# Attention of a two-part transformer block on one core: two heads per item, scores on row halves, values in column halves, outputs written in place, and one chain for both kinds of attention in layer 2

## The reference, cut to what matters

```python
# dilated (layer 1)
scores = einsum('bdhnqe,bdhnke->bdhnqk', qb, kw) * e ** -0.5   # and -inf outside the pattern
p = exp(scores - mx); den = sum(p); o = einsum('bdhnqk,bdhnke->bdhnqe', p, vw) / den
# windowed (layer 2)
p = exp(s - m); p = p / (sum(p) + exp(sk - m)); o = einsum('bnhgqk,bnkhd->bnqhgd', p, vb)
# neighbourhood (layer 2)
p = softmax(s + bias); o = einsum('bhqrk,brkhd->bqhd', p, vr)
# each followed by a product with an output matrix; q and k are normalised over their 64 values before
```

## Time and profile before

| | |
|---|---|
| median of 3 runs | 2544.2 us (2543.84 to 2547.39) |
| profiled execution, its own time | 2548.99 us |
| its span in the trace | 2547.3 us |
| TensorE matmul busy | 2474.9 us, 97% |
| VectorE busy | 1314.4 us, 52% |
| ScalarE busy | 929.2 us, 36% |
| dilated attention in the trace | from 74 to 352 us |
| both attentions of layer 2 | from 1134 to 1359 us |

### The profile page before, as it was taken

One profiled execution on the slowest core, in us unless ns is written; L12 is line 12 of the kernel. 1 busy time (PEld: TensorE's weight loads), 2 busy tenths in 40 slices (PEclk: granted clock), 3 DMA queues, 4 the chain that ended last, 5 costly groups with the idle time before them and its releaser, 6 DMA issues.

```text
span 2547.3 us, 32783 instructions
## 1 busy us (share of the span) xinstructions
PE 2474.9 (97%) x12740; PEld 1943.1 (76%) x12740; DVE 1314.4 (52%) x2069; ACT 929.2 (36%) x1463; POOL 55.0 (2%) x131
## 2 busy tenths in 40 slices
PE   8999999988999999999999999999999999999999
PEld 6777777776788888876667888887777876888887
DVE  5555555666654433557556443355565465534433
ACT  5433454334433322445445332243232232423322
POOL 3000000000000000040000000000000000000000
PEclk9999999999999999999999999999999999999999
DMA  4222213211223323320102333332222221433332
GB/s 147 70 64 64 70 60 91 62 59 51 91 91 102 97 91 99 99 87 22 46 30 92 99 99 91 95 103 83 67 67 83 75 70 34 120 94 105 92 96 76
DMA packets 60640, 205.79 MB, mean 81 GB/s; under 512 B 7249, under 2 KB 7249, under 8 KB 60386
## 3 DMA queue, kind: packets, MB, share of 16 engines
q1 hardware_dynamic: 59760, 202.93, 26.0%
q10 hardware_dynamic: 754, 1.14, 0.2%
HBM read 201.94 MB, written 2.10 MB: 80 GB/s over the span
## 4 chain that ended last, share of the span: by engine, by line
PE 88%; DVE 6%; ACT 4%; issue 1%; DMA 0%; SPq 0%; DVEq 0%; ACTq 0%
PE psum L1433 75%; PE psum L1480 2%; PE psum L1462 1%; PE psum L1516 1%; PE psum L1473 1%; PE psum L1458 1%; PE psum L1538 1%; PE psum L1543 1%; PE psum L1508 1%; PE psum L1561 1%; DVE stage L925 0%; ACT tmp L610 0%; ACT tmp L612 0%; DVE arena L1079 0%; PE psum L1528 0%
## 5 line engine op out<-in xcount | busy, mean ns | idle before, releaser
L1433 PE MATMUL psum<-hhi,whi 128*128 128x512 f32 x1640 | 656.5, 400 | 19.0 <-DVE wlo L894 9.2
L1433 PE MATMUL psum<-hlo,whi 128*128 128x512 f32 x1640 | 664.1, 405 | 0.0
L1433 PE MATMUL psum<-hhi,wlo 128*128 128x512 f32 x1640 | 652.5, 398 | 0.0
L1433 PE MATMUL psum<-uhi,whi 128*128 128x512 f32 x1392 | 554.5, 398 | 6.8 <-DVE hlo L965 2.1
L1433 PE MATMUL psum<-ulo,whi 128*128 128x512 f32 x1392 | 550.7, 396 | 0.0
L1433 PE MATMUL psum<-uhi,wlo 128*128 128x512 f32 x1392 | 546.7, 393 | 0.0
L894 DVE TENSOR_TENSOR wlo<-raw,whi 128x1024 fp32r<-128x1024 f32 (+1 forms) x399 | 465.2, 1166 | 55.9 <-ACT whi L859 29.1
L1433 PEld LDWEIGHTS psum<-hhi,whi 128*128 128x128 f32 x1640 | 313.0, 191 | 88.8 <-issue 18.0
L1433 PEld LDWEIGHTS psum<-hhi,wlo 128*128 128x128 f32 x1640 | 312.8, 191 | 74.0 <-issue 9.4
L1433 PEld LDWEIGHTS psum<-hlo,whi 128*128 128x128 f32 x1640 | 313.0, 191 | 70.5 <-issue 8.9
L859 ACT CAST whi<-raw 128x1024 fp32r<-128x1024 f32 x190 | 199.6, 1051 | 351.9 <-PE psum L1433 351.9
(11 more groups left out here) (199 smaller groups left out, 1810.5 us busy)
## 6 DMA issues: line engine op xcount, KB each, us to landing
raw<-in_packed_dram SPq DMA_DIRECT2D x359, 512.0 KB, 3.6
raw<-in_packed_dram SPq DMA_DIRECT2D x40, 256.0 KB, 2.6
x<-in_xt_dram SPq DMA_DIRECT2D x8, 256.0 KB, 7.6
out_dram<-x SPq DMA_DIRECT2D x8, 256.0 KB, 2.0
arena<-in_near_bias_dram ACTq DMA_DIRECT2D x1, 1024.0 KB, 5.7
vec<-in_vec_dram ACTq DMA_DIRECT2D x1, 44.0 KB, 4.3
arena<-in_gla_gate_up_dram ACTq DMA_DIRECT2D x1, 32.0 KB
arena<-in_gla_gate_bias_dram ACTq DMA_DIRECT2D x1, 2.0 KB
```

Of the source, the lines that this page charges most:

```text
L1433: mm = pe.matmul(g, w[:, u % 4, k, :], v[:, k, :], start=n == 0, stop=n == 3 * kt - 1)
```

## The change

- An item is now two heads (a pair) and one block of 128 queries: 16 dilated, 16 windowed, 16 neighbourhood items.
- Scores of the two heads are issued alternately: head 0 on rows 0 to 63 of the array into bank 2, head 1 on rows 64 to 127 into bank 3. The next item's scores wait until VectorE has read this item's (`att_sm`, g instead of three items back).
- VectorE adds the bias for both heads in one instruction, and takes both maxima in one. The factor 1/8 is folded into the norm gains of the queries once at the start.
- The probabilities are normalised before they are transposed: `normalise` waits for the exponential, takes the reciprocal and multiplies the whole probabilities of both heads. `turn` now waits for it (`att_norm`).
- `turn` transposes both heads into banks 4 and 5, and one ScalarE copy takes both.
- `use` has 64 value columns of each head as the stationary operand, and 128 probability columns moving. Head 0 writes partitions 0 to 63 of MB, head 1 partitions 64 to 127. The output is thus already transposed.
- ScalarE (`head_hi`) and VectorE (`head_lo`) write its high and low part (128x128) straight into the operand of the output matrix. `heads_out` and its buffers are gone. The units of the output matrix wait for each pair at the product that first needs it.
- Layer 1: an item takes four parts over two units: scores with softmax and exponentials, use of the item before, then in the next unit normalise, and turn.
- Layer 2: one run "even" of 32 items in the order windowed 0, 1, neighbourhood 0, windowed 2, neighbourhood 1, windowed 3, neighbourhood 2, 3 (four items each). 28 steps lie in the 12 units of pairs 0 to 3 (2, 2 and 3 steps in turn), the last 7 in the 8 units of the first half of the output matrix.

```diff
+    def dilated(p):
+        s = 4 * p
+        out = [[("att", "dil", s, 1)], [("att", "dil", s, 0)], [("att", "dil", s, 2), ("att", "dil", s, 3)]]
+        for i in range(s + 1, s + 4):
+            out += [[("att", "dil", i, 0), ("att", "dil", i, 1)], [("att", "dil", i, 2), ("att", "dil", i, 3)]]
+        return out
...
-    todo += beside(pair(0) + pair(1), [("att", "win", i) for i in range(32 + ATT["win"][1])])
-    todo += [(None, [("heads_out", 0, i)]) for i in range(4)]
...
+    even = [("att", "even", i) for i in range(32 + 3)]
+    todo += beside(pair(0) + pair(1) + pair(2) + pair(3), even[:28])
+    todo += beside(w_out_e(0), even[28:])
     todo += [(s, None) for s in w_out_e(1)]
...
 ScalarE
+            def exponentials(g):
+                act.wait_ge(att_max, g + 1)
+                for i in range(2):
+                    if it["kind"] == "win": ... nc.scalar.activation(c[:, 4 + i:5 + i], sinks[:, h:h + 1], ACT.Exp, ...)
+                    ins = nc.scalar.activation(p[:, i, :], p[:, i, :], ACT.Exp, bias=..., accum_out=c[:, 2 + i:3 + i])
+                ins.then_inc(att_exp, 1)
+            def head_hi(g):
+                act.wait_ge(att_pv, g + 1)
+                nc.scalar.copy(o, src).then_inc(att_hi, 1)
+            (dil)  k 0: exponentials(s)   k 1: head_hi(s-1)   k 3: copy_turned(s)
+            (even) head_hi(s-3), copy_turned(s-2), exponentials(s)
...
 VectorE
+            def normalise(g):
+                dve.wait_ge(att_exp, g + 1)
+                dve.reciprocal(c[:, 6:8], den).then_inc(dve_step, 1)
+                dve.tensor_tensor(p, p, part, ALU.mult).then_inc(att_norm, 1)
+            def head_lo(g):
+                dve.wait_ge(att_hi, g + 1)
+                dve.tensor_tensor(o, src, top.bitcast(F32), ALU.subtract).then_inc(att_lo, 1)
+            (dil)  k 0: softmax(s)   k 1: head_lo(s-1)   k 2: normalise(s)
+            (even) normalise(s-1), softmax(s), head_lo(s-3)
...
 TensorE
+            def scores(g):
+                pe.wait_ge(att_sm, g)
+                for i, r in enumerate(HALF):
+                    mm = pe.matmul(psum[:, 2 + i, 0:it["width"]], it["q"][r], it["k"][i], start=True, stop=True)
+            def turn(g):
+                pe.wait_ge(att_norm, g + 1)
+            def use(g):
+                pe.wait_ge(att_copy, g + 1)
+                pe.wait_ge(att_lo, g)
+                for c in range(2):
+                    for j in range(4):
+                        for i, r in enumerate(HALF):
+                            mm = pe.matmul(MB[r, 32 * j:32 * j + 32], v[0:w1, j, 1 + c, E * i:E * i + E], pt[0:w1, i, o:o + 32], ...)
+            (dil)  k 0: scores(s)   k 1: use(s-1)   k 3: turn(s)
+            (even) scores(s), use(s-3), turn(s-2)
```

More of the change, by code:

```diff
@@ L346, in build @@
         n_v = [place(NT, P) for _ in range(2)]
[L347 to L350, removed]
+        win_dist, win_bias = place(3 * P), place(2, 3 * P)
+        e_p = [place(2, 3 * P) for _ in range(3)]
+        e_pt = [place(2, 3 * P) for _ in range(2)]
         sinks, sinks_neg = place(8), place(8)
@@ L383, in build @@
[L383 to L386, removed]
+                items.append(dict(run="dil", kind="dil", p=p, n=n, lo=lo, w0=w0, w1=w1, width=w0 + 2 * w1, at=0,
+                                  q=d_q[buf].rearrange("p g (j l) -> p g j l", j=4), k=d_k[buf],
+                                  v=d_v[buf].rearrange("p t (g c) -> p t g c", g=GROUPS),
+                                  unit=UNIT_OF["turn", "w_in", 0, 4096 + P * p]))
@@ L387, in build, with windowed @@
+        def windowed(p):
             for n in range(NT):
                 lo, hi = max(n - 1, 0), min(n + 2, NT)
+                kv = p // 2
                 items.append(dict(
[L390 to L398, removed]
+                    run="even", kind="win", p=p, n=n, width=(hi - lo) * P, at=0, q=e_q[:, p, P * n:P * n + P],
+                    k=[(e_k if kv == i else e_k2)[HALF[i], P * lo:P * hi] for i in range(2)],
+                    bias=win_bias[:, :, P * (lo - n + 1):P * (hi - n + 1)],
@@ L399, in build, with neighbours @@
+                    blocks=[(slice(0, P), [e_v[:, b, E * kv:E * kv + E]] * 2) for b in range(lo, hi)],
+                    unit=UNIT_OF["turn", "w_in_e_2", 0, VA]))
+        def neighbours(p):
             for n in range(NT):
@@ L402, in build @@
                 bias = near_first if n == 0 else near_last if n == NT - 1 else near_bias
-                v, pt = n_v[p % 2][:, :, E * (h % 2):E * (h % 2) + E], e_pt[len(items) % 2]
                 rows = [slice(64, P) if n == 0 else slice(0, P), slice(0, 64) if n == NT - 1 else slice(0, P)]
+                v = n_v[p % 2]
                 items.append(dict(
[L406 to L409, removed]
+                    run="even", kind="near", p=p, n=n, width=hi - lo, at=64 if n == 0 else 0,
+                    q=n_q[p % 2][:, P * n:P * n + P], k=[n_k[p % 2][HALF[i], lo:hi] for i in range(2)],
+                    bias=bias[:, 2 * p:2 * p + 2, :],
+                    blocks=[(rows[b], [v[rows[b], (n + b) % NT, E * i:E * i + E] for i in range(2)]) for b in range(2)],
+                    unit=UNIT_OF["turn", "w_in_e_2", 0, VB + P * p]))
@@ L410, in build @@
+        run_at["even"] = len(items)
+        for what, p in ((windowed, 0), (windowed, 1), (neighbours, 0), (windowed, 2), (neighbours, 1), (windowed, 3),
+                        (neighbours, 2), (neighbours, 3)):
+            what(p)
         run_n = {r: sum(it["run"] == r for it in items) for r in run_at}
         for it in items:
-            it["p"] = e_p if it["run"] != "dil" else d_p
-            it["pt"] = e_pt if it["run"] != "dil" else d_pt
+            it["ps"], it["pts"] = (e_p, e_pt) if it["run"] != "dil" else (d_p, d_pt)
```

487 lines of the change are left out of this document (215 added, 272 removed).

## The result

The changed kernel takes 2531.28 us (median of 5 runs, 2526.92 to 2533.04) against 2543.86 for the kernel before (5 runs, 2542.94 to 2547.39). The ratio is 0.9946, with a 95% interval of 0.9931 to 0.996: faster by 12.6 us, where 8.5 us slower was forecast. The profiled execution took 2531.53 us, with a span of 2529.8.

A forecast was written before the change was run, and what follows sets the result against it. TensorE was taken as the bound, at work 97% of the span. Layer 1's +21.5 us and layer 2's -13 sum to +8.5, 2557.5 profiled, so a median of 2553 us; own range 2537 to 2569, 8 in 10 within 2510 to 2579.

The forecast's parts named there:

- Over 16 pairs that is -8 us: Layer 1, TensorE's scores and use: 2.75 us a pair against 3.24, taking full overlap of row halves.
- Sum +28: Layer 1, TensorE's new waits at turn for normalised probabilities: 17.5 us in pairs 0 to 2, 10.5 in gate units.
- 17.5 us: Layer 1, waits at turn in pairs 0 to 2: 5.85 us a pair, nearly all in the first three items.
- Half clock: TensorE slowed behind waits: +4 us in layer 1's gate units, +5 (bounds 0 and +20) in layer 2.
- 16 x 4.9: Layer 2, serial chain of softmax, exponentials, normalise: 16 windowed steps of 4.9 us on the mean.
- 12 x 3.4: Layer 2, the same serial chain for neighbourhood pairs, without sink: 12 steps of 3.4 us.
- 4 x 12.7: Layer 2, what stands ahead of the parts and lengthens the chain at each unit: 12.7 us per three units.
- the first half of the output matrix ... 37: Layer 2, end of stage: four steps of 3.4 + 2.05 us and four units near 4, together 37.
- A: Rival: TensorE stays the bound in layer 2, 158 us instead of 215, up to -57: 2496 us; chance 0.18.
- B: Rival: layer 1's waits at turn don't show, VectorE's post earlier or TensorE later: 2521 us; chance 0.14.
- C: Rival: row halves don't run side by side, +10 us in layer 1, nothing in windowed layer 2: 2563; chance 0.12.
- D: Rival: half clock at head units in both stages, +15 us in layer 2, +8 in layer 1: 2576; chance 0.14.

The follow-up runs named there:

- e1: Changed kernel with layer 1's normalisation done right behind split_lo, ahead of the post or the gate's logarithm: 2503.6 us, 0.9836 of the kernel before.
- e7: Changed kernel with the score matmuls of layer 2 issued twice: 2533.9 us, 0.9957 of the kernel before.
- e2: Changed kernel with VectorE doing softmax of an item before normalise of the item before it, in layer 2 alone: 2506.3 us, 0.9845 of the kernel before.
- e6: Changed kernel with one more exponential of 128 columns ahead of each head's exponential in layer 2: 2542.4 us, 0.9993 of the kernel before.
- e4: Changed kernel with normalise ahead of the post in layer 1, softmax first and a unit's first normalise ahead of the post in layer 2: 2477.1 us.
- e9: e4 with one more exponential of 96 columns per head in layer 2: 2480.7 us, 0.9745 of the kernel before.
- e10: e4 with the score matmuls of layer 2 issued twice: 2489.3 us, 0.9781 of the kernel before.
- e8: Changed kernel with both score matmuls of an item on rows 0 to 63 (head 0 twice, head 1 left out): 2542.4 us, 0.9987 of the kernel before.

## Why the prediction was wrong

It named the right mechanisms, with the right sign in each layer, and failed in sizes: 8 us too much for layer 1 and 17 too little gained in layer 2. Against the medians the miss is 21.7 us and not 26, for the reason given with the marks. The difference of two terms of opposite sign (+21.5 and -13) is what decided between faster and slower. Term by term:

- **Layer 1, work: right, and heads_out too small.** "Over 16 pairs that is -8 us": TensorE's time for scores and use (between the starts of the products on either side, less a product step of 0.23 and idle time) fell from 50.4 to 42.4 us, -8.0. heads_out gave about -4.5 in place of -2.5: the row that the forecast used ends at 358.5 us, and the last four transposes (359.70) and a wait of 1.21 us for their low part (ended at 362.66) lie behind it.
- **Layer 1, waits: "Sum +28" was 24.6** (the 26.2 of e1, less 1.6 for the clock). "17.5 us" in head units were 12.8 us of idle time (nine waits of 1.18 to 1.81), "together 10.5" in gate units 8.7 (1.73 to 2.69); the fourth item of pairs 0 to 2 had none. What failed is the place of the post. For the second and third item of a pair the exponentials end 0.6 us before the evacuation, so that ScalarE's square is done at 1.35 and not behind 1.9, and the post starts at 4.05 to 4.17. For the first item they end 0.5 to 0.6 us behind it, the square is done at 2.0 to 2.07 and the post starts at 4.67 to 4.81. The forecast had 4.56 plus a delay of 0.3 to 0.45. In the second item the post is also the short form, 0.75 us as shown above, where I had the 1.17 of the earlier trace rows for all. TensorE's place was off too, in place of 5.05: 5.3 to 5.4 us for the first item, which shortens the wait, and 4.65 to 4.83 for the others, which gives some of it back.
- **Half clock: smaller.** One of the four gate waits was followed by it: 3.5 us at 0.52, 1.6 lost in place of 4. The longest, 2.69 us, was not: the stretch behind it has 1.00. In layer 2 two head units ran for 6.9 us each at 0.51 and 0.52. The first lost 1.0 us (its shared matmul took 2.05 us where it takes 1.02 at the full clock), the second about 1.1 (10.50 us from addition to addition and 4.27 for the next, against 9.55 and 4.14 in e7, where no low stretch lies there). That is 2.1 in place of the 5 I took: much of the low stretch fell into idle time. A third stretch of 3.4 us, at 1289.5, isn't priced.
- **Layer 2, the chain: right in kind.** e2, e6 and e7 show it each in its own way. "16 x 4.9": the windowed steps took 5.15 (384 columns) and 4.14 to 4.28 (256), together 74.8 us in place of 78.4. "12 x 3.4": 2.87 (192 columns) and 3.37 (256), 37.4 in place of 40.8. "4 x 12.7" for what stands ahead of the parts: 51.0 with the half clock, against 50.8. From the first addition to the first one beside the output matrix it is 164.9 us in place of 173 and 5 for the clock.
- **Layer 2, "the first half of the output matrix ... 37": two errors.** From that addition (1317.28) to TensorE's last product of the eight units (the next unit's starts at 1344.96) it is 27.7 us. First, I let the serial chain bind here too, at 3.4 + 2.05 us per step (with four units near 4 that adds up to 37.8, written as 37). The four units with additions took TensorE 18.4 us (1315.00 to 1333.37) in place of 21.8, and it was never idle. The additions of VectorE and the scores of TensorE, after:

```profile
1317.28 0.55 DVE L1128 TENSOR_TENSOR arena<-psum,arena 128x384 f32<-128x384 f32 x1
...
1322.17 0.68 DVE L1128 TENSOR_TENSOR arena<-psum,arena 128x512 f32<-128x512 f32 x1
...
1327.25 0.69 DVE L1128 TENSOR_TENSOR arena<-psum,arena 128x512 f32<-128x512 f32 x1
...
1332.34 0.55 DVE L1128 TENSOR_TENSOR arena<-psum,arena 128x384 f32<-128x384 f32 x1
```

```profile
1316.47 0.60 PE L1518 MATMUL psum<-arena 64*128 64x192 f32 x4
...
1320.94 0.70 PE L1518 MATMUL psum<-arena 64*128 64x256 f32 x4
...
1325.51 0.70 PE L1518 MATMUL psum<-arena 64*128 64x256 f32 x4
...
1330.23 0.60 PE L1518 MATMUL psum<-arena 64*128 64x192 f32 x4
```

  VectorE comes round every 5.0 us, TensorE every 4.6. The chain is the slower one, as reckoned, but TensorE has slack at the start and loses only 0.4 us of it per step; the run ends before it is used up. Second, and larger, the two terms overlap: TensorE began the output matrix at 1311.81, 5.5 us before the addition at which the 173 ends, and the sum counts these 5.5 us twice.
- **Layer 2 in all.** The stage that was to take 215 us took 227.7 - 30.4 = 197.3. Ahead of the first addition it has 4.7 us that the sum left out; the chain with its clock is 13.1 shorter (steps 8.1, of it 1.1 for the windowed bias, the work ahead of the parts 1.9, the clock 2.9, each rounded); the output matrix is 9.3 shorter.

**The rivals.** A (TensorE bound, 2496) does not hold for the kernel that was measured: idle 26 us there, and e7. But it holds by and large for e4 (e9 and e10), whose layer 2 is 29 us shorter, half of A's 57. B (waits at `turn` don't show) is false, 21.5 us of them. C (no overlap) is false by e8; its price of +10 for layer 1 was near (9.1), its "nothing" for layer 2 was 6. D (half clock in both stages) is false: 0.99 over layer 1's attention and 0.95 over the pairs' units.

**The two rules.** The Trainium skill (TensorEngine Tiling (Array Packing), "Performance Considerations") warns that tiling speeds up TensorE and not the evacuation of PSUM, which may become the bound. In layer 2 the trace agrees in that TensorE is no longer the bound (26 us idle), but not in the cause: VectorE is busy for only 113.7 of 168 us there, and e2, which changes no amount of work, takes 24.6 us off. The Trainium skill (TensorE: Matmul & The Clock Gate, Part 3) has 3.07 times for four row tiles, less than full overlap. No run here has four; two row halves gave 1.65 in busy time, and layer 1's work came out at the sum that assumed full overlap.

## What to carry to other kernels

When an operation is moved from behind a matmul chain to ahead of it (here the normalisation), its place in the other engine's queue has to move too: here three reorderings on VectorE, with no instruction added or removed, were worth four times the change itself (54.2 against 12.6 us). When a serial chain is longer than the bound engine's step, ask how many steps it lasts and how much slack there is at its start, before its excess is charged, and whether the next stretch of the sum has already begun when the chain ends. And when a forecast is the difference of two large terms, its sign is no firmer than the weaker term: read each duration from the form that will run, not from the first row of its line.

## What the runs showed of the hardware that was not expected

- Two fp32 score matmuls of depth 64 on rows 0 to 63 and 64 to 127, in different banks, cut TensorE's busy time from 40.5 to 24.6 us (128 matmuls) and from 15.7 to 9.7 (256).
- A wait doesn't settle the clock: behind one of 2.23 us the granted clock was 0.52, behind one of 2.69 us it was 1.00, in two gate units of the same stage.
- The lower clock can lie inside the wait: from 1159.6 to 1166.5 it was 0.51, while TensorE stood idle until 1162.31, and it cost about 1 us and not 3.4. In e7 it lay only behind the wait (1163.2 to 1166.6), and the same stretch from addition to addition was 10.85 us in both.
